# Four weight slots at four distances from the activations, where all had one

## The reference, cut to what matters

```python
u = rms_norm(x, g) @ w_in            # 2048 x 4352, block one
y = concat([y_a, y_b, y_c]) @ w_out  # 2048 x 2048
up = h @ w_up                        # 2048 x 11264
f = (silu(gate) * val) @ w_down      # 5632 x 2048
# block two: w_in 2048 x 11272, w_branch_m and w_branch_a 1024 x 2048 each,
# w_out 2048 x 2048, w_up 2048 x 8192, w_down 8192 x 2048
```

## Time and profile before

| | |
|---|---|
| median of three runs | 2474.86 us |
| the profiled execution, its own time | 2448.36 us |
| span of the profile | 2446.3 us |
| TensorE busy | 2423.2 us (99%), 20658 matmuls |
| TensorE weight loads busy | 2397.1 us (98%) |
| VectorE busy | 1636.8 us (67%) |
| ScalarE busy | 1191.3 us (49%) |
| DMA | 459.51 MB, 188 GB/s on average |

### The profile page before, as it was taken

How to read it: one execution, slowest core, us unless ns; L and a number is a source line. 1 busy time by engine, 2 the same in 40 slices (tenths; PEclk the granted TensorE clock), 3 DMA queues, 4 the chain that set the end, 5 groups by cost and what they waited for, 6 DMA issues and landing times. The chain is left out here.

```text
span 2446.3 us, 48723 instructions
## 1 busy us (share of the span) xinstructions
PE 2423.2 (99%) x20658; PEld 2397.1 (98%) x20658; DVE 1636.8 (67%) x2119; ACT 1191.3 (49%) x1453; POOL 40.1 (2%) x35
## 2 busy tenths in 40 slices
PE   9999999999999999999999999999999999999999
PEld 9999999999999999999999999999999999999998
DVE  8998587665776477687767655554866565555554
ACT  6445565444554355665644444445543443443444
POOL 0000100000000000100000000001000000000001
PEclk9999999999999999999999999999999999999999
DMA  9565546555555555556555566665465655555653
GB/s 292 166 199 173 190 164 198 184 192 192 189 194 194 196 189 189 181 164 190 174 183 179 173 187 192 189 194 198 156 209 189 194 197 194 190 192 197 197 190 104
DMA packets 308075, 459.51 MB, mean 188 GB/s; under 512 B 14789, under 2 KB 156370, under 8 KB 307922
## 3 DMA queue, kind: packets, MB, share of 16 engines
q1 hardware_dynamic: 304112, 456.34, 57.5%
q10 hardware_dynamic: 3810, 0.94, 0.2%
HBM read 455.15 MB, written 2.11 MB: 187 GB/s over the span
## 5 line engine op out<-in xcount | busy, mean ns | idle before, releaser
L1712 DVE TENSOR_TENSOR w_split<-raw,w_split 128x1024 fp32r<-128x1024 f32 (+1 forms) x856 | 1044.9, 1223 | 766.7 <-ACT w_split L1122 765.4
L1122 ACT ACTIVATE w_split<-raw 128x1024 fp32r<-128x1024 f32 x853 | 901.1, 1060 | 1072.3 <-PE ps L688 1022.4
L686 PE MATMUL ps<-h_split,w_split 128*128 128x256 f32 x3904 | 1086.9, 278 | 1.6 <-DVE w_split L1712 1.5
L687 PE MATMUL ps<-h_split,w_split 128*128 128x256 f32 x3904 | 1082.1, 277 | 0.0
L688 PE MATMUL ps<-h_split,w_split 128*128 128x256 f32 x3904 | 1082.0, 277 | 0.0
L686 PEld LDWEIGHTS ps<-h_split,w_split 128*128 128x128 f32 x3904 | 734.2, 188 | 3.8 <-DVE w_split L1712 2.7
L688 PEld LDWEIGHTS ps<-h_split,w_split 128*128 128x128 f32 x3904 | 735.3, 188 | 0.0
L687 PEld LDWEIGHTS ps<-h_split,w_split 128*128 128x128 f32 x3904 | 733.0, 188 | 0.6
L686 PE MATMUL ps<-act_split,w_split 128*128 128x256 f32 x2240 | 620.8, 277 | 1.7 <-DVE act_split L1715 1.3
L687 PE MATMUL ps<-act_split,w_split 128*128 128x256 f32 x2240 | 619.4, 277 | 0.0
L688 PE MATMUL ps<-act_split,w_split 128*128 128x256 f32 x2240 | 619.4, 277 | 0.0
(11 more groups left out here) (274 smaller groups left out, 1544.6 us busy)
## 6 DMA issues: line engine op xcount, KB each, us to landing
raw<-w_up SPq DMA_DIRECT2D x152, 1024.0 KB, 5.1
raw<-w_in SPq DMA_DIRECT2D x114, 1024.0 KB, 5.3
raw<-w_down SPq DMA_DIRECT2D x108, 1024.0 KB, 5.0
raw<-w_out SPq DMA_DIRECT2D x32, 1024.0 KB, 5.0
raw<-w_in SPq DMA_DIRECT2D x16, 512.0 KB, 5.1
raw<-w_branch_m SPq DMA_DIRECT2D x8, 1024.0 KB, 5.3
raw<-w_branch_a SPq DMA_DIRECT2D x8, 1024.0 KB, 5.3
outT<-x SPq DMA_DIRECT2D x7, 256.0 KB, 2.1
```

The source lines that it names most:

```text
L686: nc.tensor.matmul(out, hi[:, cols], rhs[:, k, 0:T], start=start, stop=False)
L687: nc.tensor.matmul(out, hi[:, cols], rhs[:, k, T:2 * T], start=False, stop=False)
L1122: nc.scalar.activation(split_home(n)[0], raw[:, slot, half:half + 1024], ACT.Copy).then_inc(hi_ready, 1)
L1712: return nc.vector.tensor_tensor(out, a, b, op)
```

## The change

The one buffer `w_split` becomes four buffers, `w_split0` to `w_split3`. A table `SLOT_GAP` of 0, 16, 16 and 0 bytes goes ahead of them. A gap below 32 bytes is made by a longer buffer whose first four values stay unused; the next buffer then begins at the next multiple of 32. By the built program the data of the slots begin at 128, 144, 176 and 192 modulo 256, and the activations at 96. From slot to activations that is 224, 208, 176 and 160 modulo 256; it was 192 for all four. From stationary to moving operand in `token_chunk` it becomes 32, 48, 80 and 96; it was 64. The early buffers stay at 192 from the activations. `x` and what lies behind it move by 32 or 64 bytes.

Each engine has the same instructions in the same order as before: 15230 on TensorE's list, 2214 on VectorE's, 1805 on ScalarE's, 449 on SyncE's and 65 on GpSimd's. Only the addresses in them differ, so no rows of order are shown.

```diff
+        SLOT_GAP = (0, 16, 16, 0)
+
...
-        w_split = place("w_split", [128, SPLIT_SLOTS, 2, 1024], f32r)
-        w_hi, w_lo = w_split[:, :, 0, :], w_split[:, :, 1, :]
+        w_split = []
+        for slot in range(SPLIT_SLOTS):
+            region(SLOT_GAP[slot] // 32 * 32)
+            skip = SLOT_GAP[slot] % 32 // 4
+            w = place(f"w_split{slot}", [128, 2048 + skip], f32r)[:, skip:skip + 2048]
+            w_split.append(w.rearrange("p (a n) -> p a n", a=2))
+        w_hi, w_lo = [w[:, 0, :] for w in w_split], [w[:, 1, :] for w in w_split]
         x = place("x", [128, KT, T])
-        STAGGER = 192
-        region(STAGGER)
+        STAGGER = 224
+        region((w_split_at + STAGGER - top[0]) % 256)
...
-            return w_hi[:, slot, :], w_lo[:, slot, :]
+            return w_hi[slot], w_lo[slot]
...
-            return w_split[:, (n.base - 4) % SPLIT_SLOTS, :, :]
+            return w_split[(n.base - 4) % SPLIT_SLOTS]
...
```

More of the change, by code:

```diff
@@ L460, in split_home @@
                     slot = (n.base - 2 * early) % SPLIT_SLOTS
-                    return w_hi[:, slot, :], w_lo[:, slot, :]
+                    return w_hi[slot], w_lo[slot]
             slot = n.base % SPLIT_SLOTS
-            return w_hi[:, slot, :], w_lo[:, slot, :]
+            return w_hi[slot], w_lo[slot]
         def split_pair(n):
-            return w_split[:, (n.base - 4) % SPLIT_SLOTS, :, :]
+            return w_split[(n.base - 4) % SPLIT_SLOTS]
         def gate_home():
-            return w_split[:, (G2 - 4) % SPLIT_SLOTS, :, :].rearrange("p a (k n) -> p (a k) n", n=128)
+            return w_split[(G2 - 4) % SPLIT_SLOTS].rearrange("p a (k n) -> p (a k) n", n=128)
         def freed_by(n):
@@ L1183, in _ @@
             for half, signal in enumerate((first_hi, hi_ready)):
-                nc.scalar.activation(w_hi[:, 0, 512 * half:512 * half + 512], raw[:, 0, 512 * half:512 * half + 512],
+                nc.scalar.activation(w_hi[0][:, 512 * half:512 * half + 512], raw[:, 0, 512 * half:512 * half + 512],
                                      ACT.Copy).then_inc(signal, 1)
@@ L1851, in _ @@
                 dve.wait_ge(ready, 1)
-                tt(w_lo[:, 0, cols], raw[:, 0, cols], w_hi[:, 0, cols].bitcast(f32), ALU.subtract).then_inc(signal, 1)
+                tt(w_lo[0][:, cols], raw[:, 0, cols], w_hi[0][:, cols].bitcast(f32), ALU.subtract).then_inc(signal, 1)
             dve.wait_ge(x_loaded[1], 16)
```

## The result

The changed kernel took 2525.73 us, the median of four runs that lie within 1.1 us (2525.61 to 2526.65). The kernel before took 2478.22 us over its four runs beside them (2461.56 to 2481.75). The ratio is 1.0261, with a 95% interval of 1.0214 to 1.0308: slower by 2.6%, where the prediction had 2440 us and a range up to 2525. Ratios here leave out runs over 1.5% above the fastest of the same kernel (of the kernel before 1 of 7 and 3 of 13 further on), so they are not the quotients of the medians beside them. The profiled execution took 2525.69 us, so its profile stands for the median; that of before was 26.5 us under the median at the time. From profile to profile the span grew by 77.3 us, from 2446.3 to 2523.6.

A forecast was written before the change was run, and what follows sets the result against it. The prediction took TensorE's matmul stream to bound the kernel. From the profiled 2448.4 us it took 17 us for ended slow stretches and added 8.5 us for settling: 2440 us, range 2380 to 2525.

The forecast's parts named there:

- The bound: Whole kernel: TensorE busy for 2423.2 of 2446.3 us at 2.4 GHz, so the time is that of the matmul stream.
- The writes of ScalarE and VectorE, costed at nothing: High-part and rest writes go to other addresses; even 10% more, 104 us on VectorE, fits in its 766.7 us idle.
- The two cadences: Same matmuls in the kernel before run at a slow or a fast pace, near 117.8 and 113.3 ns, 4.5 apart.
- the term called decisive: Four distances in turn, shifting every 24 matmuls, should end slow stretches: 433 us of them, 17 us to gain.
- the prediction's sum: Profiled execution 2448.4 us, less 17 for slow stretches, plus 8.5 for changes of slot: 2440 us.
- settling: At each change of slot, at most 0.02 us, 17 us for some 850 pieces; half taken, 8.5 us.
- no slow stretch: The profiled execution without its slow stretches, some 3,700 matmuls at 4.5 ns each, would take 2431 us.
- slow at the new distances: Rival: all 19,200 matmuls of `whole_tile` run at 117.8 ns, 2431 + 19,200 x 4.5 ns = 2518 us; chance 0.27.
- Its sign: In the profile after, 120 us windows would hold 1000 to 1025 matmuls all through.
- the upper end: Price of a matmul at a new distance, from `token_chunk`: 106.7 + 12.5 = 119.2 ns, 5.9 more than fast.
- Nothing happens: Rival: distance modulo 256 plays no part and both paces stay; 2448 to 2482 us, middle 2475; chance 0.26.
- The 109.2 ns: Warm matmul spacing by the skill's columns / 2.4 + 2.5 ns; by it the kernel would take an estimated 2352 us.

The follow-up runs named there:

- one64: The whole kernel with its four slots at 192, 192, 192 and 64 bytes from the activations, against the kernel before: 2439.29 us, ratio 0.9942.
- the two coarse sweeps: Matmuls alone, both blocks left out, at 16 distances from 0 to 240, activations at 64, then at 96; 192 took 113.3 or 117.8 ns with activations at 64.
- the three sweeps: Matmuls alone, both blocks left out: 16 distances with activations at 64, the same at 96, then 64 distances in 4-byte steps; lowest 113.3 ns.

## Why the prediction was wrong

- **The bound was right.** The time is the pace of the stream. The writes of ScalarE and VectorE, costed at nothing, cost nothing.
- **The two cadences were right.** Their part in the spread is likely, but not shown: `one64`, which has the fast one nearly alone, does not spread, and one profile of before has both in one execution. None was taken of a slower run of before, so that these have more of the slow cadence is inferred.
- **The step that failed** is the term called decisive: "Now every 24 matmuls the pattern shifts, in some way like an interruption. A slow stretch of a thousand matmuls should then not last." The slow cadence gave way only to cadences that the new distances have. I had taken for granted that those would include 113.3 ns. In the two coarse sweeps 224, 208, 176 and 160 never went below 117.3, while 192 can. Changing the distance takes the kernel out of the two-cadence state into one of 118.4 ns all through, where the prediction's sum had 113.3. The step was to take 17 us off and to put 8.5 on for settling; the split products took 83 us more.
- **As a rule the step holds for some distances only.** Between 192 and 64, which both have the fast cadence, the change does end the slow one, and once settled the borders cost nothing: 192, 64, 192, 64 is then at 113.33 ns to the last piece. But 192, 192, 192, 208 stayed in the slow cadence through every border when it was entered slow (117.9 ns), and 0 or 240 among three 192 ended the fast one. That the forecast's 2440 us is the time of `one64` is luck: the change does not have its distances, and the terms of the sum do not match either. `one64` lies 8 us over the 2431 of no slow stretch; from profile to profile its split products take 10 us less than before, not 17, and `token_chunk` 2 us more.
- **The rival "slow at the new distances"** is what happened. It had 0.27 and 2518 us. Its mechanism was right and its term too small: it used 117.8 ns, the slow cadence of 192, where the mean came to 118.39. With 5.1 instead of 4.5 ns it is 2431 + 19,200 x 5.1 ns = 2529 us; some 480 other matmuls of this pace add 2 us and the rest is 5 us shorter, which makes 2526. Its sign came too: windows of 1000 to 1025 matmuls all through (1016).
- **The evidence in the rows was thin.** The only other distance in the trace, that of `token_chunk`, was costlier, and it spoke for this rival. It was right by luck: it came from 64, which with the usual operands turned out to have the fast cadence. Nor was its 119.2 ns the upper end it was called, as all slots at 208 ran at 123.2 for thousands of matmuls.
- **"Nothing happens"** falls, and with it what was cited for it. "SBUF — State Buffer", section "SBUF: two separate sides", in the Trainium skill says that TensorE waits for no one at its port, and "TensorE: Matmul & The Clock Gate", Part 2, that a weight load takes nothing from a running matmul. Here the same matmuls take 113.3 to 123.3 ns by nothing but the distance of their two operands and their entry, and the measurement decides. The 109.2 ns that the prediction estimated from Part 1 of "TensorE: Matmul & The Clock Gate" in the Trainium skill was not reached at any of 64 distances.
- **What stays open** is the rule behind the table. No run shows whether it is reads that get in each other's way, and which, or why one combination of entry and distance settles at 113.3 and another at 117.8.

## What to carry to other kernels

Where TensorE is busy for the whole time, divide stretches by their matmuls before asking what waits: two paces for the same code are a cost that no wait shows, and a cause of spread between runs. The address distance of the two operands is worth a sweep with matmuls alone, which holds all distances in one run, but with many entries to each, since one entry shows one cadence of several (204 looked fast behind both of its two). Before mixing distances, know the cadences of each: mixing two that share a fast one removed the slow one here (0.5 to 0.6% of the time, and the spread), and mixing four without it cost 2.6%.

## What the runs showed of the hardware that was not expected

- 128 by 128 weights against 256 columns in `float32r` settle at a steady pace between 113.3 and 123.3 ns, with the clock at 2.4 GHz throughout. Of the 256 stretches of the three sweeps 77 were at 120.0 or 120.1, 39 at 118.3, 30 at 117.8, 29 at 116.7 and 14 at 113.3. The best is 6.6 ns over 256 columns at that clock.
- The pace depends on the distance of the operands to 4 bytes, modulo 256 as far as tried: behind the same products it was 119.6 and 119.2, 117.8 and 113.3 ns at 196, 200 and 204.
- A pace once entered holds for thousands of matmuls: 113.4 ns for 5783 of the kernel before from 1773 to 2428 us, 123.2 ns for the same ones with all slots at 208. In the profiles of before, of all slots at 208 and of all slots at 204, none of the uninterrupted stretches of over 400 matmuls changed its pace once settled.
- Shifting only one of the three products of a tile mostly loses the fast pace: 13 of the 14 combinations that shift one did, behind two small products each. The other had the rest of the weights at 64.
